# Two spacer tiles resized: where the activation buffers and the weight ring start within 64 bytes

## The reference

```python
def swiglu_ffn(x, w_gu, w_down):
    gate, up = jnp.split(x @ w_gu, 2, axis=-1)
    return (jax.nn.silu(gate) * up) @ w_down
```

## Time and profile before

| | |
|---|---|
| median of three runs | 2692.09 us |
| the profiled execution | 2694.12 us |
| its span, first to last instruction | 2692.0 us |
| mean granted TensorE clock | 0.987 |
| HBM read | 442.86 MB, 165 GB/s over the span |
| weight load (PEld) busy | 90% of the span |
| DMA engines, stream queue | 49.0% of 16 engines' span |

### The profile page before, as it was taken

One profiled execution on the slowest core, in us unless ns is written; L12 is line 12 of the kernel. 1 busy time (PEld: TensorE's weight loads), 2 busy tenths in 40 slices (PEclk: granted clock), 3 DMA queues, 4 the chain that ended last, 5 costly groups with the idle time before them and its releaser, 6 DMA issues.

```text
span 2692.0 us, 51716 instructions
## 1 busy us (share of the span) xinstructions
PE 2613.1 (97%) x18604; PEld 2410.1 (90%) x18604; DVE 1920.5 (71%) x3131; ACT 1502.9 (56%) x2579; POOL 201.6 (7%) x280
## 2 busy tenths in 40 slices
PE   8999799999999999999999999999999999999998
PEld 7998699999998899999998998989989999988997
DVE  7777676778777576777777667777787776676876
ACT  6556556556555656556555555655565555555554
POOL 0001001000000201000000160000000005300000
PEclk9999899999999999999999999999999999999999
DMA  7554244655554344555654543545545545335553
GB/s 261 202 189 135 87 134 156 225 202 183 186 187 157 102 158 136 188 186 169 204 187 142 179 157 103 165 154 185 186 154 187 187 143 171 126 118 165 172 187 109
DMA packets 122821, 445.80 MB, mean 166 GB/s; under 512 B 13688, under 2 KB 14712, under 8 KB 122688
## 3 DMA queue, kind: packets, MB, share of 16 engines
q1 hardware_dynamic: 120816, 436.79, 49.0%
q0 software_dynamic: 1872, 7.17, 0.7%
HBM read 442.86 MB, written 1.05 MB: 165 GB/s over the span
## 4 chain that ended last, share of the span: by engine, by line
PE 92%; DVE 5%; ACT 2%; issue 1%; DMA 0%; SPq 0%; ACTq 0%; DVEq 0%
PE bank L457 91%; DVE w_lo L1471 1%; PE bank L808 1%; DVE rt L1699 1%; DVE z L1537 1%; ACT w_hi L1037 0%; DVE rt L1493 0%; DVE x L1530 0%; DVE a L1498 0%; ACT score L1271 0%; DMA x<-in_x_dram 0%; DVE rstd_x L1490 0%; DMA raw<-in_stream_dram 0%; ACT L1245 0%; DVE z L1643 0%
## 5 line engine op out<-in xcount | busy, mean ns | idle before, releaser
L457 PE MATMUL bank<-a,w_hi 128*128 128x256 f32 (+1 forms) x5360 | 1342.3, 329 | 38.5 <-DVE a L1498 38.0
L1471 DVE TENSOR_TENSOR w_lo<-raw,w_hi 128x1024 fp32r<-128x1024 f32 x829 | 1016.7, 1230 | 278.3 <-ACT w_hi L1037 277.1
L457 PE MATMUL bank<-a,w_lo 128*128 128x256 f32 x3736 | 1013.2, 282 | 0.0
L457 PEld LDWEIGHTS bank<-a,w_hi 128*128 128x128 f32 x5360 | 897.4, 190 | 126.2 <-issue 45.7
L1037 ACT CAST w_hi<-raw 128x1024 fp32r<-128x1024 f32 x829 | 858.0, 1046 | 42.6 <-DMA raw<-in_stream_dram 35.4
L457 PE MATMUL bank<-b,w_hi 128*128 128x256 f32 (+1 forms) x4096 | 859.5, 301 | 3.6 <-DVE b L1498 2.6
L457 PEld LDWEIGHTS bank<-a,w_lo 128*128 128x128 f32 x3736 | 709.2, 190 | 16.8
L457 PEld LDWEIGHTS bank<-b,w_hi 128*128 128x128 f32 x4096 | 656.9, 188 | 40.6 <-issue 3.5
L457 PE MATMUL bank<-b,w_lo 128*128 128x256 f32 x2400 | 658.6, 280 | 0.0
L457 PEld LDWEIGHTS bank<-b,w_lo 128*128 128x128 f32 x2400 | 450.4, 188 | 5.6
L1084 ACT COPY pt<-bank 128x256 f32<-128x256 f32 x176 | 65.5, 372 | 219.1 <-PE bank L457 219.1
(11 more groups left out here) (185 smaller groups left out, 2130.7 us busy)
## 6 DMA issues: line engine op xcount, KB each, us to landing
raw<-in_stream_dram SPq DMA_DIRECT2D x829, 512.0 KB, 3.3
z<-in_biasc_dram POOLq DMA_DIRECT2D x6, 512.0 KB, 4.5
z<-in_biasa_dram POOLq DMA_DIRECT2D x3, 512.0 KB, 4.4
x<-in_x_dram SPq DMA_DIRECT2D x2, 512.0 KB, 8.0
v<-in_mem_dram POOLq DMA_DIRECT2D x2, 512.0 KB, 6.3
out_dram<-x SPq DMA_DIRECT2D x8, 128.0 KB, 1.9
con<-in_con_dram POOLq DMA_DIRECT2D x1, 912.0 KB, 6.6
vec<-in_vec_dram POOLq DMA_DIRECT2D x1, 417.0 KB, 5.6
```

The costliest lines, as they stand in the source:

```text
L457: return nc.tensor.matmul(out, lhsT, rhs, start=start, stop=stop, skip_group_check=shared)
L1471: return nc.vector.tensor_tensor(out, a, hi.bitcast(F32), ALU.subtract)
```

## The change

Two spacer tiles change their size. Nothing else in the program does: no instruction, wait or transfer is touched.

```diff
         raw = sb("raw", [P, RAW, D])
-        sb("gap_a", [P, 4])
+        sb("gap_a", [P, 8])
         a_two, b_two = sb("a", [P, C, 2, T], F32R), sb("b", [P, C, 2, T], F32R)
         a_hi, a_lo = a_two[:, :, 0, :], a_two[:, :, 1, :]
         b_hi, b_lo = b_two[:, :, 0, :], b_two[:, :, 1, :]
-        sb("gap_x", [P, 12])
+        sb("gap_x", [P, 8])
         x = sb("x", [P, C, T])
```

## The result

The changed kernel takes 2722.7 us (median of 4 runs, 2722.1 to 2724.7) against 2691.9 us before (4 runs): ratio 1.0109, 95% interval 1.0096 to 1.0121. It is slower by 31 us. The forecast was no effect, 2692 us. The time lies inside the range of 2656 to 2730 us, near its upper end and near the low price of rival 2, 2727 us.

The account below looks back on a forecast made before the run. The prediction took PE's matmul beat as the bound, with PE on 92% of the chain. Every term was 0, giving 2694.1 us for the profiled execution, 2692 by the median; range 2656 to 2730 us.

Parts of the forecast that it names:

- rival 2: PE: ring at 0 beside activations at 32 slows blocks 1.9 to 4.5 ns; low price 2727 us, high 2775; chance 0.28.
- What really moves: SBUF placement: `a` and `b` stay at remainder 32; the ring and other tiles come down 32 bytes to 0.
- Rival 3: Placement: `a` and `b` go from 16 to 32 as the text says, all else at 0; either sign; chance 0.02.
- ScalarE, VectorE, DMA: Casts, splits and first load of `x`: each term 0, with ends of 0.1, 1.3 and 0.3 us either way.
- theory X: Expectation set for follow-up runs, not in the prediction: `x`, `z`, `score` and the like at 0 cost the time.
- TensorE: Matmul operand reads on PE: new remainders change the block beat by nothing; taken as 0 between -72 and +83 us.
- sign of rival 2: Trace after, down tile: a round of three blocks passing 0.356 us would show the prediction wrong by rival 2.
- three beats: Matmul blocks with tiles of one remainder run at 113.3, 115.6 and 117.8 ns; taken as an argument for a small effect.
- rival 1: PE's two operand streams come apart and meet less, so faster: full price -72 us, 2620; half, 2656; chance 0.22.
- The rules: PE's operand reads: 16-byte lines mean nothing changes; stationary loads take no bandwidth; the isolated-gap rule allowed up to -147 us.

Follow-up runs that it names:

- run with two distances: Full kernel at distance 64 modulo 256, but the feed-forward stages' normalised input starts 32 bytes lower, against the kernel before: 2674.3 us, ratio 0.9930.

## Why the prediction was wrong

*What really moves.* Right: `a` and `b` stayed where they were, and the ring moved by 32 bytes. The run with the ring alone moved gives 2721.4 us. Rival 3, the text taken at its word, had nothing in it.

*ScalarE, VectorE, DMA.* Right: cast 1045 ns, split 1229 ns, each within 1 ns of before; the 0.4 us more in the load of `x` is just over its bound of 0.3. What theory X stood for is worth a few us at most.

*TensorE.* This is the step that failed: a term taken as 0 between -72 and +83 us measured +31 us. The prediction's own sign of rival 2 came, a down round at 0.360 us, over its 0.356. The place was right: the cost lies between the two operands that PE reads. Rival 2's condition was not: a ring at 0 beside activations at 32 modulo 64 is also what the run with the ring 32 bytes up has, and that is faster than before. Its low price was near by luck. 31 us / 18,408 is 1.7 ns a block where it had 1.9, but not on every block: the down tile grew by 1.9 ns a block and the gate and up tiles by 0.3.

What misled me was the sentence "with equal remainders there are three beats, so something other than the remainder sets them". The runs show that the beat depends on the form of the tile, on one common distance and on the tiles ahead, so three beats at one distance say nothing against it. I also took the wrong modulus. By remainders modulo 64 a move by 32 bytes has one outcome; by 256 the kernel stood at 192, and 32 bytes down it takes 2722 us, 32 up 2689 and 128 up 2673.

*The argument against rival 1* ("with the ring moving, both streams are at 32 too, and still 4.5 ns of it are gone") had the clue: the same remainders gave another beat once the roles were exchanged. At 192 the ring-moving tile has its stationary operand 64 above the moving one, a distance at which PE alone ran the down tile at 113.3 ns too (as it did at 192). It went to 118.9 ns after the change.

*The rules.* The Trainium skill, "SBUF — State Buffer" (section "Specifications (TRN2)", cachelines), has lines of 16 bytes and a penalty for each crossing into a new one. That alone would have nothing change for a move by 32 bytes. With ratios from 0.992 to 1.011 over moves in multiples of 32 bytes, it doesn't tell all that a start costs. The Trainium skill, "TensorE: Matmul & The Clock Gate" (section "Step-by-step: what each phase is for"), says that loading the next stationary operand takes no SBUF read bandwidth from the running matmul. With PE alone the down tile ran at 113.3 to 120.0 ns a block by where the stationary operand stood from the moving one, so for this type and these shapes the two reads are not independent in time. The prediction also held its beats against the gap of an isolated matmul. These are rows of matmuls with a load each, so no disagreement follows from that.

*What stays open.* What in the memory has a period of 256 bytes is not shown. Nor is it shown what picks a rhythm. The ring-moving tile takes 2.818 us in the run with the ring alone moved and 2.850 in the changed kernel, both at 160, with ring and activations at the same addresses and only other tiles moved; these are the two values that PE alone has for that distance read as stationary less moving, 96. The down tile at 64 finds its fast rhythm in the full kernel and not with PE alone in the same order. The run with two distances shows only that the tile ahead can decide it; that other engines have a part in it is not excluded.

## What to carry to other kernels

Where a chain lies on PE without idle time, compare the distance of matmul starts with the column time; what is left over may hang on the addresses of moving and stationary operand. Try the distance between the two tiles in steps of 32 bytes up to 256, in the full kernel and by its median: of the seven distances tried here in the full kernel the best (64) gained 0.8% and the worst cost 1.1%. A table with PE alone gave the size of the effect and not always the rhythm of a tile. Check that all parts of an operand have the same distance modulo 256. Look up the addresses that a program was given before believing its spacer tiles.

## What the runs showed that I had not expected

- A matmul of 256 float32r columns beside a load of 128 costs 113.3 to 120.0 ns at a granted clock of 1.00, with no other engine at work, by the distance of its operands modulo 256 bytes and by the tiles ahead; 256 columns at 2.4 GHz are 106.7 ns.
- The sign of the distance is stationary less moving: in steps of 32 bytes, a tile with exchanged roles has the values of the mirrored distance.
- 16-byte steps count: with PE alone a round takes 8.52 us at 0, 8.38 at 16 and 8.49 at 32.
- The rhythm is handed on: the same down tile at the same distance took 2.720 us behind its like and 2.829 us behind pair tiles, with no other engine at work.
- No other engine is needed for the effect: at 160 the down tile took 2.874 us in the full kernel and 2.880 with PE alone, the single tile 2.880 in both. Rounds still differed by up to 0.11 us (at 64).
